# Layer 0's modulation behind the first 16 tiles: from rows on TensorE to sums on VectorE

## What is computed

```python
def first_block(x, c, positions, ada_w, ada_b, ...):
    cond = jax.nn.silu(c)                                     # 1 x 1024
    for layer in range(2):
        mod = (cond @ ada_w[layer] + ada_b[layer])[:, None, :]   # 1 x 6144
        sh1, sc1, g1, sh2, sc2, g2 = jnp.split(mod, 6, axis=-1)
        h = rms_norm(x, norm_mix_g[layer]) * (1.0 + sc1) + sh1
        x = x + g1 * hybrid_mixer(h, positions, w_in[layer], ..., w_out[layer])
        h = rms_norm(x, norm_ffn_g[layer]) * (1.0 + sc2) + sh2
        x = x + g2 * (swiglu(h, ...) if layer == 0 else moe_swiglu(h, ...))
    return rms_norm(x, final_g)

def hybrid_mixer(h, positions, w_in, ..., w_out):
    gq, gk, gv, gr, ga, rq, rk, rv, rg = jnp.split(h @ w_in, ...)
    o_g = gla_core(gq, gk, gv, log_sigmoid(ga @ w_alpha + b_alpha) / 16)   # norm, silu(gr)
    o_r = retention_core(rotary(rq), rotary(rk), rv, log_gamma)            # norm, silu(rg)
    return concatenate([o_g, o_r]) @ w_out
```

## Time and profile before

| | |
|---|---|
| median of 3 runs | 3051.75 us (3050.82 to 3053.11) |
| the profiled execution | 3045.71 us, span of its instructions 3043.9 us |
| TensorE busy | 2904.1 us, 95% of the span |
| VectorE busy | 1839.4 us, 60% |
| ScalarE busy | 1197.1 us, 39% |
| mean granted clock of TensorE | 0.972 of full speed |

### The profile page before, as it was taken

The page is one execution under the profiler, slowest core; times in us unless marked ns, Lnnn a source line. Parts: engine busy times, 40 slices in busy tenths (PEclk is TensorE's granted clock), DMA queues, the critical chain, the costliest instruction groups (busy, mean ns, idle before and its releaser), DMA issues.

```text
span 3043.9 us, 42647 instructions
## 1 busy us (share of the span) xinstructions
PE 2904.1 (95%) x17305; PEld 2498.7 (82%) x17305; DVE 1839.4 (60%) x2914; ACT 1197.1 (39%) x1723; POOL 0.2 (0%) x4
## 2 busy tenths in 40 slices
PE   6999999989999999899999999999999999989999
PEld 5889998879998677688887777888878888877998
DVE  4657778655546566576575365554547757656554
ACT  4345453444444444422223344422224222245544
POOL 0000000000000000000000000000000000000000
PEclk9999999979999999899999999999999999999999
DMA  9738766366777777465461212444434636422564
GB/s 309 257 118 237 225 216 202 125 191 194 227 208 288 274 302 290 111 185 159 141 203 49 80 63 56 135 135 114 144 96 144 199 111 182 129 80 79 154 178 131
DMA packets 557033, 511.40 MB, mean 168 GB/s; under 512 B 14307, under 2 KB 533542, under 8 KB 556710
## 3 DMA queue, kind: packets, MB, share of 16 engines
q1 hardware_dynamic: 477350, 390.56, 41.7%
q10 hardware_dynamic: 79488, 118.11, 12.1%
HBM read 507.57 MB, written 1.05 MB: 167 GB/s over the span
## 4 chain that ended last, share of the span: by engine, by line
PE 86%; ACT 5%; DVE 4%; DMA 2%; issue 1%; SPq 1%; ACTq 0%; DVEq 0%
PE bank L751 24%; PE bank L753 23%; PE bank L752 23%; PE bank L1002 3%; PE bank L895 2%; DMA weights_raw<-in_moe_w 2%; ACT ring L1568 2%; PE bank L1466 1%; PE bank L1457 1%; PE bank L779 1%; PE bank L951 1%; PE bank L953 1%; PE bank L952 1%; DVE weights_split L2029 1%; PE bank L1478 1%
## 5 line engine op out<-in xcount | busy, mean ns | idle before, releaser
L751 PE MATMUL bank<-hn_split,weights_split 128*128 128x256 f32 (+1 forms) x3008 | 1015.4, 338 | 62.2 <-DVE hn_split L2075 34.0
L752 PE MATMUL bank<-hn_split,weights_split 128*128 128x256 f32 (+1 forms) x3008 | 998.3, 332 | 0.0
L753 PE MATMUL bank<-hn_split,weights_split 128*128 128x256 f32 (+1 forms) x3008 | 997.9, 332 | 0.0
L2029 DVE TENSOR_TENSOR weights_split<-weights_raw,weights_split 128x1024 fp32r<-128x1024 f32 (+2 forms) x520 | 673.2, 1295 | 226.5 <-ACT weights_split L1514 225.7
L1514 ACT ACTIVATE weights_split<-weights_raw 128x1024 fp32r<-128x1024 f32 (+2 forms) x520 | 577.7, 1112 | 569.5 <-PE bank L753 528.7
L751 PEld LDWEIGHTS bank<-hn_split,weights_split 128*128 128x128 f32 x3008 | 583.7, 194 | 141.8 <-issue 69.4
L752 PEld LDWEIGHTS bank<-hn_split,weights_split 128*128 128x128 f32 x3008 | 584.2, 194 | 51.3 <-issue 1.9
L753 PEld LDWEIGHTS bank<-hn_split,weights_split 128*128 128x128 f32 x3008 | 583.2, 194 | 51.5
L751 PE MATMUL bank<-hidden_split,weights_split 128*128 128x256 f32 (+1 forms) x1144 | 382.0, 334 | 0.0
L753 PE MATMUL bank<-hidden_split,weights_split 128*128 128x256 f32 (+1 forms) x1144 | 380.0, 332 | 0.0
L752 PE MATMUL bank<-hidden_split,weights_split 128*128 128x256 f32 (+1 forms) x1144 | 379.8, 332 | 0.0
(11 more groups left out here) (405 smaller groups left out, 2855.9 us busy)
## 6 DMA issues: line engine op xcount, KB each, us to landing
weights_raw<-in_w_ffn_in SPq DMA_DIRECT2D x176, 512.0 KB, 5.2
ada_halves<-in_w_ada ACTq DMA_DIRECT2D x96, 768.0 KB, 4.8
weights_raw<-in_moe_w SPq DMA_DIRECT2D x80, 704.0 KB, 6.5
ada_halves<-in_ada_w ACTq DMA_DIRECT2D x54, 768.0 KB, 4.9
weights_raw<-in_moe_w SPq DMA_DIRECT2D x66, 512.0 KB, 5.3
weights_raw<-in_w_in SPq DMA_DIRECT2D x60, 512.0 KB, 5.5
expert_down<-in_moe_w SPq DMA_DIRECT2D x25, 1024.0 KB, 5.4
weights_raw<-in_w_ffn_out SPq DMA_DIRECT2D x32, 768.0 KB, 4.8
```

The costliest lines, as they stand in the source:

```text
L751: mm(ps, wh, xh, start=first, stop=False)
L752: mm(ps, wh, xl, start=False, stop=False)
L753: return mm(ps, wl, xh, start=False, stop=last)
L2029: tt(split_view(slot, 1, kts, n), raw, split_view(slot, 0, kts, n).bitcast(F32), ALU.subtract)\
```

## The change

Layer 0's eleven chunks take the way of layer 1's. `AdaTurns` gets an entry "in1.0" with 33 tiles; `in_modulation`, the copy of the row and the combined addition go. VectorE now does `sum_quarter` for each quarter, at the end of the turn that `sum_at` names: chunks 0 to 6 have their quarters in turns 0, 1, 2, 2 of each three (counted from turn 3c), chunk 7 in turns 21, 22, 24, 26, chunk 8 in 27, 27, 28, 29, chunk 9 in 30, 30, 31, 32 and chunk 10 in 33, 33, 34, 34. (Turn 29 + m is unit m of out1.0.) TensorE's three sums of a chunk follow two turns after its last quarter: behind units 4, 7, 10, 13, 16, 19, 22 and 28 of in1.0 and units 2, 5 and 7 of out1.0. The columns lie where those of tiles 16 to 23 were, so ahead of chunk 3's sums TensorE waits until VectorE has added the bias to tiles 16 to 23, at the end of turn 12; tiles 24 to 47 get theirs behind out1.0. Loads of the halves are issued by `ada_parts` at the end of ScalarE's turns, the first two after the copies of the first modulation, as before.

```diff
 class AdaTurns:
-                turns, _, self.n = FFN[name] if name in FFN else (1, SEQ, 24)
-                self.name, self.conds = name, 1 if name in ("ffn1.0", "in1.1") else 2
+                turns, _, self.n = FFN[name] if name in FFN else (1, SEQ, 24 if name == "in1.1" else 33)
+                self.name, self.conds = name, 1 if name in ("in1.0", "ffn1.0", "in1.1") else 2
...
-                if name == "in1.1":
+                if name[:3] == "in1":
                     self.sums = [[RAW[:, i, 2048:2048 + ADA_COLS]] for i in range(2)]
-                    self.sum_at = [2 + q + (q >= 20) for q in range(4 * self.per)]
+                    if name == "in1.1":
+                        self.sum_at = [2 + q + (q >= 20) for q in range(4 * self.per)]
+                    else:
+                        last = [1 + 3 * c for c in range(8)] + [28, 31, 34, 36]
+                        self.sum_at = [last[c] - 1 + j * (last[c + 1] - last[c]) // 4 for c in range(11) for j in range(4)]
+                        for c in range(11):
+                            self.sum_at[4 * c + 3] = last[c + 1] - 2
                     self.load_at = [0 if q < 2 else self.sum_at[2 * q - 3] + 1 for q in range(2 * self.per)]
...
 TensorE
-            def in_modulation(i):
-                c, h = (i - 2) // 2, i % 2
-                if h == 0 and 1 <= c <= IN_CHUNKS:
-                    pe.wait_ge(ada_copied, c)
-                    ada_columns(ADA_COLS + 15 + 3 * (c - 1), AROW, ADA_TILES, 1)
-                if 0 <= c < IN_CHUNKS:
-                    pe.wait_ge(ada_half[h], 16 * (c + 1))
-                    ada_half_rows(4, CONDP1, h)
...
             def ada_sums(g, x, p):
                     if p == x.sum_at[4 * c + 3] + 2:
                         if c == 0:
                             pe.wait_ge(mod_ready, g + x.mods)
+                        if x.name == "in1.0" and c == 3:
+                            pe.wait_ge(mod_ready, x.mods + 1)
...
-                    if layer == 0:
-                        in_modulation(i)
...
-                    if layer and i < 28:
-                        ada_sums(0, ADA["in1.1"], i)
+                    if i < 28:
+                        ada_sums(0, ADA[name], i)
...
 ScalarE
-                    for h in range(2):
-                        act.wait_ge(ada_used, h + 1)
-                        act.dma_start(AH[:, h, :, :], in_view[0, h]).then_inc(ada_half[h], 16)
+                    ada_parts(0, ADA["in1.0"], 0)
...
-                    c, h = (i - 3) // 2, (i - 3) % 2
-                    if layer == 0 and 0 <= c < IN_CHUNKS:
-                        act.wait_ge(ada_used, 2 * c + h + 3)
-                        if c + 1 < IN_CHUNKS:
-                            act.dma_start(AH[:, h, :, :], in_view[c + 1, h]).then_inc(ada_half[h], 16)
-                        if h == 1:
-                            act.wait_ge(ada_done, 4 + c)
-                            act.activation(AROW[:, :], PS[4][:, 0:ADA_COLS], ACT.Copy).then_inc(ada_copied, 1)
...
-                    if layer and i:
-                        ada_parts(0, ADA["in1.1"], i)
+                    if i:
+                        ada_parts(0, ADA[name], i)
...
 VectorE
-                    if layer:
-                        mixer_sums(i)
+                    mixer_sums(ADA[name], i)
                     if layer == 0 and i == 9:
                         angles()
+                    if layer == 0 and i == 12:
+                        dve.wait_ge(ada_done, ADA["in1.0"].done(0, 2))
+                        tt(MOD1[:, 16:24], PS[4][:, 1:9], col("ada_b", 16, 8), ALU.add).then_inc(mod_ready, 1)
...
-                if layer == 0:
-                    dve.wait_ge(ada_done, 4 + IN_CHUNKS)
-                    tt(MOD1[:, 16:48], PS[4][:, ADA_COLS + 16:ADA_COLS + 48], col("ada_b", 16, 32), ALU.add)\
-                        .then_inc(mod_ready, 1)
                 gla_scale()
                 dve.wait_ge(mod_ready, 2)
-                out_phase(f"out1.{layer}", T, lambda m, s: mod(2, m), (lambda m: mixer_sums(29 + m)) if layer else None)
-                if layer:
-                    x = ADA["in1.1"]
-                    dve.wait_ge(ada_done, x.done(0, x.per - 1))
-                    tt(MOD1[:, 72:96], PS[4][:, 0:24], col("ada_b", 72, 24), ALU.add).then_inc(mod_ready, 1)
+                out_phase(f"out1.{layer}", T, lambda m, s: mod(2, m), lambda m, x=ADA[name]: mixer_sums(x, 29 + m))
+                x = ADA[name]
+                dve.wait_ge(ada_done, x.done(0, x.per - 1))
+                c0, p0 = (72, 0) if layer else (24, 9)
+                tt(MOD1[:, c0:c0 + 24], PS[4][:, p0:p0 + 24], col("ada_b", c0, 24), ALU.add).then_inc(mod_ready, 1)
```

31 lines of the change are left out of this document (15 added, 16 removed).

## The result

The changed kernel is slower: against the kernel before, 13 runs of each, the ratio is 1.0035 with a 95% interval of 1.0025 to 1.0045, so 10.7 us more (7.6 to 13.7). Its median is 3060.3 us, that of the kernel before 3049.4 in these runs.

What follows compares the result with a forecast made beforehand. TensorE was 86% of the chain, with VectorE short of room at both ends of layer 0's mixer. Terms 4.0 + 1.0 - 9.6 + 1.2 + 1.1 + 4.8 = +2.5 us on 3051.75 gave 3054.2 us, range 3044 to 3063.

Steps and rivals of the forecast that it cites:

- The likeliest case: Whole kernel: within about 0.2% of before, 3045.6 to 3057.9 us, chance 0.60; the forecast's sum was +2.5 us.
- rival 3: Halves of the weights land late, 1.4 us more for each of four: +5.6 us, 3060 us; chance 0.10.
- Stretch 1: Units 2 to 13 of in1.0: VectorE's queue delays unit 14 by 4.0 us, plus 1.0 us for the clock.
- the gate's 2.5 us that stay empty: Units 2 to 13: of VectorE's 3.68 us wait on ScalarE's gate chain, 2.5 us can't be filled with quarters.
- The 15.0 us of idle time to be filled: Units 2 to 13: of VectorE's 19.0 us idle, 15.0 take new work, 16.1 with 0.09 us a gap.
- The low clock: Units 2 to 13: after long waits TensorE's matmuls run at half speed; +1.0 us, bounds 0 and 3.2.
- Stretch 2: Units 14 to 25: TensorE sheds ten blocks (7.8 us) and three column groups (1.8), 13 quarters fit: -9.6 us.
- Handover and first residual: Units 27 and 28 into out1.0: quarters ahead of the last split cost +1.2 us, ahead of the gated output +1.1.
- Out1.0: First to last residual: nine quarters need 10.2 us, 5.4 of it covered by VectorE's idle time; +4.8 us.
- Rival 1: VectorE hides all the new work, TensorE's 17.2 us and a 1.2 us wait go: 3033 us; chance 0.12.
- The 9.4 us "less work": Units 2 to 13: TensorE loses the first 12 modulation blocks, 9.4 us, and spends that time waiting.
- Rival 2: Units 8 to 14: TensorE falls to 1.2 GHz and stays there, about 6 us more: 3060 us; chance 0.18.

Runs made afterwards that it cites:

- add_late: Changed kernel with VectorE's addition for tiles 16 to 23 in turn 14 instead of 12, chunk 3's sums behind unit 15 instead of 13; 1.0024 against before.
- no_sums: Changed kernel with 66 of its 88 new VectorE instructions left out, loads, signals and TensorE's sums kept; ratio 0.9960 against the kernel before.
- late_free: Changed kernel with chunks 4 to 10 at two quarters a turn in turns 12 to 26, none in turns 27 to 34; ratio 1.0035 against before.
- after_again: The changed kernel unaltered, profiled a second time; mixer 6.5 us longer than the kernel before, one run.
- spread_pool: Changed kernel with early quarters one a turn, seven quarters in out1.0, addition in turn 16, halves' loads issued from GpSimd's queue; ratio 0.9985 against before.
- tail_moved: early_moved with 28 quarters in turns 14 to 26, up to three a turn, and four behind; ratio 1.0025 against the kernel before.
- early_moved: spread_pool with the twelve early quarters in turns 0 to 7 and 11 to 13, none in turns 8 to 10; ratio 0.9965 against the kernel before.

## Why the prediction was right or wrong

The time lies inside the range, 3044 to 3063 us, near its upper end. The likeliest case, no change, was not what came: the loss is clear of noise, the side that had 0.27. The mixer's +6.1 and +6.5 lie in the case's own range of -4 to +8; the 10.7 us of the whole kernel do not, and for what lies behind the mixer the sum had no term. That the time is still inside is owed to the width of the range. Of the signs, the kind was right and the size was not: unit 14 at 120.8 to 122.1 us instead of 117 to 119, unit 26 some 2 to 3 us earlier than before instead of 5, out1.0 25.25 us long instead of 23; and VectorE did wait on halves, which was the sign of rival 3. By steps:

- **Stretch 1, +5.0: measured +7.2 and +7.5.** VectorE as the limit was right, and so were the gate's 2.5 us that stay empty (2.49) and the places where TensorE waits. One term was mis-sized. The 15.0 us of idle time to be filled came out at about 12: VectorE's idle time fell from 19.0 to 6.9 us, of which 1.5 is a half that landed late, which I had only in rival 3, and some 2 are short gaps, which I had at 1. So VectorE came to its next split 69.7 us behind unit 2 instead of 62.4, 7.2 us late where I had 4.3, and unit 14 was late by as much: that it follows VectorE's delay through the new wait was right. What this wait costs by itself add_late shows: with it moved, unit 14 starts 3.2 us earlier, and the stretch is 4.0 us longer than before.
- **The low clock, +1.0.** Right in kind: it came behind the rotary turn's wait and ahead of unit 14, as named. Behind unit 14's wait it cost 1.3 us (the unit took 4.46 us instead of 3.14), which as the traces are divided falls into stretch 2; at the rotary turn VectorE was the later one anyway.
- **Stretch 2, -9.6: measured -11.1 and -10.9.** Every block counted here, and VectorE's 13 quarters were hidden. The low clock went both ways: 1.3 us were lost at unit 14, and 1.5 gained from the outputs of the first half of the mixer to unit 26 (15.85 and 15.82 us in the two traces of before, 14.28 and 14.31 in those of the change), where half speed lasted less long. So blocks and column groups are worth about 10.8 us, 1.2 more than the sum had; where that 1.2 comes from is not shown.
- **Handover and first residual, +1.2 and +1.1: measured +1.3 and +1.1.** Read from layer 1's rows, and right.
- **Out1.0, +4.8: measured 6.65 between the residuals.** 1.22 is a late half again. Behind it another 1 us goes, for which the sum had no term: the norm's sums start at half speed behind a wait of 2.50 us (1.01 us instead of 0.61). For the late halves, I had priced rival 3 by the longest landing on record and given it 0.10; it was not a case of its own but a part of the likeliest one.
- **Rival 1** fell: VectorE hid the work in the middle and not at the ends. With most of the sums left out TensorE's gain was 12 us, not 18.4; whether the rest is there without late halves and half speed stays open. The 9.4 us "less work" ahead of unit 14 was counted as if it had all been on the path. **Rival 2** was right that the clock falls behind the waits, and not that it stays low: between the rotary turn and chunk 3's wait, from 111.52 to 121.70 us, the granted clock was 1.00.
- The Trainium skill's "TensorE: Matmul & The Clock Gate", section "HAM oscillation — how this bites in real kernels", which says that bursts of matmuls between waits start at the low clock each time and which the prediction weighed as a rule for rival 2, was borne out by no_sums and late_free, where waits of 2.33 and 4.31 us were followed by half speed, and not by the changed kernel's first trace, where the decayed products ran at full speed behind a wait of 2.86 us (2.16 us for the group). Its second trace, after_again, agrees again: 3.52 us behind the same wait.

## What to carry to other kernels

Work taken from the busiest engine is worth only what of it is on the path in its stretch. A run with the new work left out shows what is left of the gain, but with the loads and waits that stay, so its traces have to be read for these too. A stretch has room for moved work only if the engine, and the buffers and loads that feed the work, both have it; with two buffers and loads of 5 to 9 us the loads ran out before VectorE did. And a wait that a moved step needs for a bank or a buffer has a price of its own, which a second place for the same step shows quickly. Last, two programs that are the same up to a point can differ there by 2 us in their traces: compare such a pair before reading a smaller difference.

## What was not expected of the hardware

The same wait did not always cost TensorE its clock, not even in the same kernel. 2.86 us ahead of the decayed products left it at 2.4 GHz in the first trace of the changed kernel (2.16 us for the group) and were followed by 1.2 GHz in the second (3.52 us), as were 2.33 us at the same place in no_sums (3.65 us) and 2.85 in spread_pool (3.32 us). So the length of that one wait does not decide it. The row of after_again:

```profile
90.74 3.52 PE L1174 MATMUL bank<-gla_products 64*128 64x128 f32 x32 [2.86 <-DVE gla_key_decayed L2489]
```

And waits cost more than their length: in tail_moved VectorE's waits for halves in the middle came to 10.3 us (the table of waits of that stretch), in early_moved to 1.2, and the stretch was 18 us longer. TensorE was idle for 8.8 us of these and busy for 9.2 us more, at a granted clock of 0.81 over 89.4 us instead of 0.93 over 71.4.
